# A projection that starts on the raw input: three half tiles summed from x before the norm is known, and scaled afterwards

## The reference, cut to what matters

```python
h = rmsnorm(x, norm_mix)                      # y = x * rsqrt(mean(x*x) + eps) * g
proj = h @ w_in + b_in                        # 5 * 1024 output channels
conv_val, conv_gate, pool_in, gate_a, gate_b = split(proj, 5)
ya = conformer_conv_branch(conv_val, conv_gate, ...)   # gate, 31-tap causal conv, layer norm, silu, matmul
yb = pool_branch(pool_in, ...)                         # trailing means over 2/4/8/16 tokens, group matmul
x = x + (sigmoid(gate_a) * ya + sigmoid(gate_b) * yb) @ mix_w_out
x = x + gdfn(rmsnorm(x, norm_ffn), ...)                # gated MLP, 2816 channels
return rmsnorm(x, norm_final)
```

## Time and profile before

| what | value |
|---|---|
| runs | 1361.4 us median of 3 (1361.03 to 1363.41) |
| the profiled execution | 1362.16 us, its span 1360.3 us |
| granted clock of TensorE, mean | 0.99 of full speed |
| busy: TensorE, VectorE, ScalarE, GpSimd | 98%, 60%, 29%, 54% of the span |

### The profile page before, as it was taken

The page is one execution under the profiler, slowest core; times in us unless marked ns, Lnnn a source line. Parts: engine busy times, 40 slices in busy tenths (PEclk is TensorE's granted clock), DMA queues, the critical chain, the costliest instruction groups (busy, mean ns, idle before and its releaser), DMA issues.

```text
span 1360.3 us, 16021 instructions
## 1 busy us (share of the span) xinstructions
PE 1336.2 (98%) x6092; PEld 1113.2 (82%) x6092; DVE 810.5 (60%) x971; ACT 399.5 (29%) x555; POOL 739.3 (54%) x502
## 2 busy tenths in 40 slices
PE   7999999999999999999999999999999999999997
PEld 6888888888888788878887888888888888888887
DVE  6799899999574545545696555454555453320225
ACT  4311221211112551111244444444444433322210
POOL 5656446554453353356947887777877714434101
PEclk8999999999999999999998999999999999999998
DMA  5111111110111112344302222222222238531003
GB/s 194 63 47 54 39 47 47 47 47 32 47 55 40 45 47 80 121 136 143 139 32 93 93 93 92 79 77 79 94 78 93 80 126 304 187 108 62 0 1 124
DMA packets 32931, 114.47 MB, mean 84 GB/s; under 512 B 3040, under 2 KB 9184, under 8 KB 28768
## 3 DMA queue, kind: packets, MB, share of 16 engines
q1 hardware_dynamic: 29328, 104.12, 22.2%
q10 hardware_dynamic: 3536, 9.44, 2.0%
HBM read 93.62 MB, written 19.92 MB: 83 GB/s over the span
## 4 chain that ended last, share of the span: by engine, by line
PE 86%; DVE 5%; DMA 2%; issue 1%; POOL 1%; ACT 1%; SPq 0%; POOLq 0%; DVEq 0%; ACTq 0%
PE ps L1366 28%; PE ps L1367 28%; PE ps L1368 28%; DMA tmp<-g_kept 2%; DVE ga_r L1216 1%; DVE tmp L1126 1%; DVE raw L1222 1%; POOL w_lo L565 0%; PE ps L1420 0%; PE ps L1430 0%; DVE ga_r L1241 0%; DVE res L1209 0%; DVE res L1207 0%; DVE res L1206 0%; DVE res L1343 0%
## 5 line engine op out<-in xcount | busy, mean ns | idle before, releaser
L1366 PE MATMUL ps<-h_lo,w_hi 128*128 128x512 f32 (+1 forms) x972 | 375.9, 387 | 8.1 <-DVE h_lo L971 6.6
L1367 PE MATMUL ps<-h_hi,w_lo 128*128 128x512 f32 (+1 forms) x972 | 373.1, 384 | 0.0
L1368 PE MATMUL ps<-h_hi,w_hi 128*128 128x512 f32 (+1 forms) x972 | 373.1, 384 | 0.0
L478 POOL TENSOR_SCALAR w_hi<-raw 128x1024 fp32r<-128x1024 f32 x66 | 72.1, 1093 | 297.9 <-issue 241.5
L1366 PEld LDWEIGHTS ps<-h_lo,w_hi 128*128 128x128 f32 x972 | 184.6, 190 | 45.7 <-DVE h_lo L971 7.4
L1367 PEld LDWEIGHTS ps<-h_hi,w_lo 128*128 128x128 f32 x972 | 184.6, 190 | 35.6 <-issue 0.5
L1368 PEld LDWEIGHTS ps<-h_hi,w_hi 128*128 128x128 f32 x972 | 184.5, 190 | 35.3
L1366 PE MATMUL ps<-ga_r,w_hi 128*128 128x512 f32 (+1 forms) x428 | 166.7, 389 | 4.0 <-POOL w_lo L565 3.0
L480 POOL TENSOR_TENSOR w_lo<-raw,w_hi 128x1024 fp32r<-128x1024 f32 x66 | 163.6, 2478 | 5.5
L1367 PE MATMUL ps<-cv_r,w_lo 128*128 128x512 f32 (+1 forms) x428 | 165.8, 387 | 0.0
L1368 PE MATMUL ps<-cv_r,w_hi 128*128 128x512 f32 (+1 forms) x428 | 165.8, 387 | 0.0
(11 more groups left out here) (193 smaller groups left out, 2011.7 us busy)
## 6 DMA issues: line engine op xcount, KB each, us to landing
raw<-in_wstream SPq DMA_DIRECT2D x68, 512.0 KB, 3.5
tmp<-in_wffn SPq DMA_DIRECT2D x16, 1024.0 KB, 4.8
tmp<-g_kept SPq DMA_DIRECT2D x22, 512.0 KB, 4.3
res<-in_wffn SPq DMA_DIRECT2D x10, 1024.0 KB, 4.7
g_kept<-res SPq DMA_DIRECT2D x14, 512.0 KB, 2.6
raw<-in_wffn SPq DMA_DIRECT2D x5, 1024.0 KB, 5.0
res<-in_xT ACTq DMA_DIRECT2D x4, 1024.0 KB, 4.9
x_kept<-res ACTq DMA_DIRECT2D x16, 256.0 KB, 2.3
```

The source lines that it names most:

```text
L478: pool.tensor_scalar(hi, r, 1.0, 0.0, ALU.mult, ALU.add).then_inc(w_hi_done, 1)
L1366: nc.tensor.matmul(out, a_hi, b_lo, start=start, stop=False, skip_group_check=onto)
L1367: nc.tensor.matmul(out, a_lo, b_hi, start=False, stop=False, skip_group_check=onto)
L1368: return nc.tensor.matmul(out, a_hi, b_hi, start=False, stop=stop, skip_group_check=onto)
```

## The change

What it does:

- **Raw first halves.** For tokens 0 to 511 (half 0, as quarters 0 and 1) ScalarE writes `h_hi` as x times gain (no factor), and VectorE `h_lo` as x times gain minus that, in one instruction with x and `h_hi` as inputs. TensorE makes the first halves of v0 and g0 (quarter by quarter) and of v1 from these. v1 goes to PSUM slot 2 (banks 4 and 5), so that three tiles stand open.
- **Scaling afterwards.** When the factor of half 0 is known, ScalarE copies it from PSUM to SBUF (`scales_kept`), and VectorE multiplies the three finished half tiles in PSUM by it.
- **The norm by halves.** Squares are taken by 1024 columns at a time and added in a tree of three (1024, 512 and 256 columns) for each quarter, all on VectorE, in the order of quarters 0, 2, 3, 1. Then half 1 is normed first, with 512 columns in an instruction, x in place in `res`; VectorE writes low halves of even k, GpSimd of odd k. Half 0 is normed later, when its raw halves have been used, for all tiles from g1 on. Its high halves of k = 4 to 7 stand behind the read-outs of g0 and v0 on ScalarE.
- **Weights.** GpSimd splits four chunks at the start, the third and fourth into `ga_r`. SyncE loads W0 before x, W2 and W3 once `raw` is free; the gain comes over ScalarE's DMA queue.
- **Order.** TensorE: v0, g0 on quarter 0; on quarter 1; v1 on half 0; v0 and g0 together on half 1; v1 on half 1; g1. The variances and broadcasts lie in between. The dummy matmuls are 16 instead of 24 and 6. The convolution waits for v1's read-out as well, since v1 lies in its banks. GpSimd's low halves of both norms come before glu0.

The diff, cut to its core:

```diff
+        n1_sq = [t[:, i * KT * PART:(i + 1) * KT * PART] for t in (tmp, cv) for i in range(2)]
+        n1_scale = [bank(6 + h) for h in range(2)]
+        scales_kept = cv[:, 5 * SEQ:5 * SEQ + HALF]
+        N_FIRST = 4
+        def first_w(n):
+            if n < 2:
+                return w_hi[:, n * CH:(n + 1) * CH], w_lo[:, n * CH:(n + 1) * CH]
+            a = (n - 2) * 2 * CH
+            return ga_r[:, a:a + CH], ga_r[:, a + CH:a + 2 * CH]
...
+            load_weights(0)
             load_x(0)
+            load_weights(1)
             load_x(1)
             load_x(2)
+            sp.wait_ge(w_split, 1)
+            load_weights(2)
             load_x(3)
             sp.dma_start(par[:, KT:], params[:, KT:]).then_inc(par_loaded, 16)
+            sp.wait_ge(w_split, 2)
+            load_weights(3)
...
-            for n in range(2):
-                split(n, n, 0)
+            for n in range(N_FIRST):
+                pool.wait_ge(raw_loaded[n % 2], 16 * (n // 2 + 1))
+                r, (hi, lo) = raw[:, n % 2 * CH:(n % 2 + 1) * CH], first_w(n)
+                pool.tensor_scalar(hi, r, 1.0, 0.0, ALU.mult, ALU.add).then_inc(w_hi_done, 1)
+                pool.wait_ge(w_hi_done, n + 1)
+                pool.tensor_tensor(lo, r, hi.bitcast(f32), ALU.subtract).then_inc(w_split, 1)
...
+            for h in (1, 0):
+                low_halves(n1[h], *span(h), None)
             for n in range(2, 2 * LOOSE):
-                split(n, n % 2, n // 2)
+                if n >= N_FIRST:
+                    split(n, n % 2, n // 2)
                 for x in BESIDE.get(n, ()):
                     beside(x[:-1], int(x[-1]))
...
+            def high_raw(p):
+                for k in range(KT):
+                    act.wait_ge(x_loaded[p][k * len(x_loaded[p]) // KT], 16)
+                    act.activation(tile(h_hi, k, *part(p)), tile(res, k, *part(p)), ACT.Copy,
+                                   scale=par1("norm_mix", k)).then_inc(raw_hi, 1)
...
+            high_raw(0)
+            squares(0)
+            high_raw(1)
+            for p in (2, 3, 1):
+                squares(p)
+            deviation(n1[1], 0, n1_scale[1])
             for k in range(KT):
+                high1(1, k)
+                if k == 4:
+                    deviation(n1[0], 8, n1_scale[0])
+            act.activation(small[:, 62:63], eps[:, :], ACT.Sigmoid).then_inc(gate_ready, 1)
+            act.wait_ge(bc_done, n1[0]["nth"])
+            act.activation(scales_kept, n1_scale[0], ACT.Copy).then_inc(scale_kept, 1)
+            act.wait_ge(raw_used, 1)
+            for k in range(KT // 2):
+                high1(0, k)
...
+            act.wait_ge(par_loaded, 16)
+            gate(0, TURN["g", 0], CHUNK["g", 0])
+            value(0, CHUNK["v", 0])
+            for k in range(KT // 2, KT):
+                high1(0, k)
+            act.wait_ge(n1[0]["lo_v"], KT // 2)
+            act.wait_ge(n1[0]["lo_p"], KT // 2)
+            act.dma_start(pw_raw, pool_w).then_inc(pw_loaded, 16)
+            for kind, i in START[2:]:
...
+            low_raw(0)
+            list(add_up(0, 0))
+            low_raw(1)
+            list(add_up(2, 1))
+            list(add_up(3, 2))
+            rest = add_up(1, 3)
+            next(rest)
+            invert(n1[1], 0, n1_diag[1])
+            list(rest)
+            normed(1, 4, lambda: invert(n1[0], 8, n1_diag[0]))
+            dve.wait_ge(scale_kept, 1)
+            dve.wait_ge(raw_used, 1)
+            for i in range(2):
+                scale(i)
             for c in range(2):
                 for odd in range(2):
                     a = c * GLW + odd * (PAD + HALF)
                     dve.memset(tmp[:, a:a + PAD], 0.0).then_inc(pads, 1)
+            normed(0)
+            scale(2)
+            for h in range(2):
+                settled(n1[h], True)
+            dve.wait_ge(par_loaded, 16)
             dve.memset(csum, 0.0).then_inc(pads, 1)
...
+                if isinstance(c, int) and c == 0:
+                    dve.wait_ge(val_out, 2)
                 dve.wait_ge(glu_done, 2 * c + 2)
...
+            keep_busy(16)
+            for p in range(2):
+                for n in range(2):
+                    pe.wait_ge(w_split, n + 1)
+                    for k in range(KT):
+                        pe.wait_ge(raw_lo, KT * p + k + 1)
+                        last = first(n, k, slot(n, *part(p)), *part(p))
+            last.then_inc(s1_half, 1)
+            pe.wait_ge(w_split, 3)
+            for k in range(KT):
+                if k == 3:
+                    variance1(1)
+                if k == 7:
+                    broadcast1(1)
+                last = first(2, k, slot(2, *span(0)), *span(0))
+            last.then_inc(raw_used, 1)
+            for k in range(KT):
+                if k == 2:
+                    variance1(0)
+                if k == 6:
+                    broadcast1(0)
+                low1(1, k)
+                for n in range(2):
+                    last = first(n, k, slot(n, *span(1)), *span(1))
+                    if k == KT - 1:
+                        last.then_inc(w_used, 1)
```

More of the change, by code:

```diff
@@ L333, in build @@
         n2_sq, n2_sum = sems("n2_sq", "n2_sum")
-        n2 = [norm(PARTS + 1 + h, ("val", "hi", "lo_v", "lo_p")) for h in range(2)]
+        n2 = [norm(3 + h, ("val", "hi", "lo_v", "lo_p")) for h in range(2)]
         x1_loaded = sem("x1_kept_most")
@@ L348, in build @@
         x2_mm, x2_done, last_gain, last_scale, last_out = sems("x2_mm", "x2_done", "last_gain", "last_scale", "last_out")
-        nf = [norm(PARTS + 3 + h, ("sq", "sum", "out")) for h in range(len(FINAL))]
+        nf = [norm(5 + h, ("sq", "sum", "out")) for h in range(len(FINAL))]
         x1_kept = nc.dram_tensor("x1_kept", (KT * P, SEQ), f32, kind="Internal").ap()
@@ L474, in split @@
                 pool.wait_ge(raw_loaded[s], 16 * (i + 1))
-                wait(pool, w_used, n - 1)
+                wait(pool, w_used, n - 3 if isinstance(n, int) and n < N_FIRST + 2 else n - 1)
                 pool.sem_inc(split_go, 1)
@@ new lines, in squares, with high1 @@
+            def squares(p):
+                act.wait_ge(x_loaded[p][-1], 16)
+                for q in range(2):
+                    x = res[:, 4 * q * SEQ:4 * (q + 1) * SEQ].rearrange("p (k n) -> p k n", k=4)
+                    a, b = part(p)
+                    act.activation(n1_sq[p][:, 4 * q * PART:4 * (q + 1) * PART].rearrange("p (k n) -> p k n", k=4),
+                                   x[:, :, a:b], ACT.Square).then_inc(squared, 1)
+            def high1(h, k):
+                act.wait_ge(n1[h]["val"], k + 1)
+                act.activation(tile(h_hi, k, *span(h)), tile(res, k, *span(h)), ACT.Copy).then_inc(n1[h]["hi"], 1)
@@ L626, in _ @@
+            act.dma_start(par[:, 0:KT], params[:, 0:KT]).then_inc(gain_loaded, 16)
             act.wait_ge(consts, 5)
             root_table()
[L628 to L643 removed]
+            act.wait_ge(gain_loaded, 16)
@@ L1439, in _, with variance1, broadcast1 @@
             pe.wait_ge(consts, 5)
-            def variance1(p):
-                squares = n1_sq[p % 2]
-                variance(bank(6 + p % 2), [((n1[p]["sum"], 5 if p == 0 else KT - 1), squares[0])], var_done, PART // P)
-            def broadcast1(p):
-                if p >= 2:
-                    pe.wait_ge(n1[p - 2]["val"], KT)
-                broadcast(n1[p], bank(4 + p % 2, 0, PART), n1_diag[p])
+            def variance1(h):
+                pe.wait_ge(tree, 12 - 3 * h)
+                for j in range(HALF // P):
+                    src = n1_sq[2 * h + j // 2][:, j % 2 * P:(j % 2 + 1) * P]
+                    last = nc.tensor.matmul(n1_scale[h][:, j:j + 1], src, mean_w[:, 0:1], start=True, stop=True)
+                last.then_inc(var_done, 1)
+            def broadcast1(h):
+                broadcast(n1[h], n1_scale[h], n1_diag[h])
             def keep_busy(n):
@@ new lines, in _ @@
+            for k in range(KT):
+                last = first(2, k, slot(2, *span(1)), *span(1))
+            last.then_inc(w_used, 1)
+            turn = TURN["g", 1]
+            pe.wait_ge(w_split, N_FIRST)
+            for h in range(2):
+                pe.wait_ge(s1_out, 2 * turn + h - 1)
+                for k in range(KT):
+                    if h == 0:
+                        low1(0, k)
+                    last = first(N_FIRST - 1, k, slot(1, *span(h)), *span(h))
+                last.then_inc(w_used if h else s1_half, 1)
```

149 lines of the change are left out of this document (45 added, 104 removed).

## The result

The changed kernel took 1366.81 us (median of 9 runs, 1364.37 to 1370.71), the kernel before, on the same chip, 1361.61 (9 runs, 1359.77 to 1364.54). The ratio is 1.0036, 95% interval 1.0023 to 1.0050: 3.1 to 6.8 us slower. The profiled execution has a span of 1366.5 us against 1360.3.

What follows compares the result with a forecast made beforehand. TensorE, busy 98%, bounds the kernel. The 3.4 us gained at p0 are lost in p2's wait, leaving p2 1.25 us later; 2.8 us of low clock make +4.1: from 1361.4 to 1365.5 us, range 1357 to 1369.

Steps and rivals of the forecast that it cites:

- Splits and held low halves: Front: GpSimd's weight splits hold Vector's raw low halves of quarter 1 until 25.2 us; alone they would end about 15.
- First broadcast: After v1's first half: done at 38.2 us with TensorE at 1.2 GHz for this piece, 34.9 at full clock.
- From there to the convolution: Second broadcast to first convolution: waits in a row on three in-order engines, 17.9 us; convolution at 68.3, 10 us later.
- p0: Start of tile p0: TensorE waits 2.5 us for GpSimd's split and starts at 71.9, 3.4 us earlier than before.
- p2: Start of tile p2: TensorE idles 4.7 us for g2's read-out, starting at 120.1, 1.25 us later than before.
- The clock behind p2: After the wait at p2: TensorE's clock falls to 0.50, costing 2.8 us.
- Nothing later: After p2: later places have room and waits from 420 us on move with TensorE, so no further cost.
- Rival 1: Front gain stays: late Vector chain hides in its room, p2 does not wait, 3.4 us kept; 1358.0; chance 0.10.
- Rival 2: GpSimd's hold of Vector is smaller: convolution at 61.8, p2 at 113.6; 1356.1, or 1358.9 with low clock; chance 0.13.
- Rival 3: Kinder clock: v1's first half at full clock, convolution at 65.0; 1359.3, or +0.7 us; chance 0.27 including its second form.
- its second form: Clock falls already at p0's 2.5 us wait, hidden by p2's wait: +1.25 us, 1362.7; chance included in Rival 3's.
- Rival 4: One more clock fall, under second halves of v0 and g0: convolution at 71.1, +6.9 us, 1368.3; chance 0.15.

Runs made afterwards that it cites:

- the first experiment: Changed kernel with ScalarE making the high halves of the pooled means behind g2's read-out, against the kernel before: 1361.73 us, ratio 0.9997.

## Why the prediction was right, and where its sizes were off

I forecast 1365.5, slower, with 0.50 for slower; it is 1366.8. Step by step:

- **Splits and held low halves.** Forecast ends of the splits: 8.0, 12.8, 20.1, 24.6; measured 8.2, 12.6, 19.8, 24.7. Last raw low half 25.4 (forecast 25.2), last sum 30.07 (30.3). The hold is as costed.
- **First broadcast.** Forecast end 38.2, of which 3.3 was a low clock under v1's first half; measured 37.07. The step failed in its place and size: the clock was down from 25.8 to 29.2, under g0's quarter 1, and at 1.00 while v1's first half ran (30.3 to 37.4). Among executions of this same front the broadcast's start ranges from 34.39 to 36.05 with the place of the low stretch, so such a fall costs up to 1.7 here. That the pauses lower the clock at all was right: with them filled it stayed up.
- **Second halves, second broadcast.** Idle 1.6 forecast, 1.53 measured; the broadcast ends at 49.84 (50.4). No clock fall came here.
- **From there to the convolution.** Forecast 17.9, measured 67.74 - 49.84 = 17.9.
- **p0.** Forecast 71.9 after a wait of 2.5; measured 71.11 after 1.92, 4.3 us earlier than the 75.42 of before (forecast 3.4, from 75.3).
- **p2.** Forecast a wait of 4.7 at 120.1 for g2's read-out; measured 4.37 at 119.32. From the convolution 51.58 (51.8), with the second mean held as foreseen. The term is 0.38 instead of 1.25: p2 came 0.8 earlier than forecast, most of it from the clock in the front, and the p2 of before is at 118.94, not at the 118.85 that the forecast worked out.
- **The clock behind p2.** 2.8 forecast; 3.06 - 0.38 = 2.7 measured, and by the dummies 2.6. The size is that of this execution: behind the same wait it was 1.4 in the run with `pads` at 4.
- **Nothing later.** This step failed in the profiled execution: I wrote that later places have room and that the last waits, from 420 us on, move with TensorE. The variance of the layer norm waits 0.67 where it waited 0.35, and a low clock of 6.8 us behind it cost 3.2. Of the nine profiles of the changed kernel and its variants with that wait of 0.67 us, three have a fall there (6.8, 3.4 and 3.4 us long); of the five with one of 0.35, the kernel before and its variants among them, two have one of 3.4. So it comes in some executions, whatever the kernel, and is no sure cost of the change. The sum without it, 0.4 + 2.7 + 0.3 = 3.4, lies at the lower end of the measured interval, 3.1 to 6.8.

  What fills the rest of the median's 5.2 stays open; that it is more such falls is argued, not shown. The same gap stands in other runs: the run with 20 dummies is 0.9 ahead of the kernel before at the wait for line 581 (728.03 against 728.89), and its median is 2.6 behind. One profile is one execution, and those of the variants lie from 3.9 below to 2.9 above their own medians, so rows of single profiles do not settle differences smaller than that. One more wait is new, 0.56 us for `res` at 756.94, and costs nothing that shows: between the wait for line 581 and the next one for it both kernels take 436.7 and 436.6 us.

The mechanism was right: the held low halves, the late convolution, ScalarE's order, the wait at p2 and the clock behind it all came as forecast, and the first experiment shows that the wait at p2 decides. That the time came out within 1.3 us of the forecast is in part luck. In the profiled execution p2 was 0.9 less late than forecast, and the later fall, put at nothing, more than made up for it.

Rival 1 failed as the forecast said, at ScalarE's order: the front gain was 4.3 at p0 and gone at p2. Rival 2, a smaller hold, was tried: without the hold the convolution starts at 64.09, not at 61.8, because the squares' sums take the low halves' place beside the splits. The rival had priced them as not held. Rival 3 came true in its place (v1's first half at 1.00) and not in its price, since the clock was down under g0 instead; its second form, the clock falling at p0, was seen in one variant's profile. Rival 4 did not come.

## What to carry to other kernels

A gain at the start passes every in-order queue before it counts: list the first waits that it runs into (here GpSimd's split at p0, ScalarE's read-out at p2) and take all of them away, since one removed alone may uncover the next (here another split, 1.6 us late). When one engine holds another, moving the holder can just move the hold to the next instructions, as it did here, where those had no time to spare. A loss of 0.36% and a gain of 0.3 to 0.4% lay three lines of order apart. And let medians decide before rows: the nine executions of the changed kernel lie 6.3 us apart, more than any single edit was worth.

## What the runs showed of the hardware

- A Vector instruction of 16 columns with two SBUF inputs lasted 2.33 us beside a GpSimd instruction of 2.42 us; 0.18 us with none beside it (at 110.18). It ended 0.03 us after the GpSimd instruction: the holder set the length of the hold, not the size of the held one. With the second input in PSUM eight low halves beside a split took 3.22 us, with both in SBUF 7.28. It goes both ways: beside Vector's sums GpSimd's two splits took 9.1 us instead of 7.0.
- Six profiles have the front of the changed kernel with its six pauses of up to 1.9 us. All six show the lower clock in it, but not at a fixed place: with the same instructions it was down from 25.8 to 29.2 in one execution, 13.7 to 17.1 in another, and in both places (12.6 to 16.0, 26.2 to 29.6) in a third. Its cost hangs on what TensorE does there: nothing where a wait for data behind it takes the lost time up, 1.7 us where TensorE is behind.
- Dummy matmuls in a wait (4.6 us of them in one of 4.4; 5.0 us spread over five waits; 17 us over the same five) had the clock at 1.00 in those waits and behind them, in each of the three kernels that had them. They must be sized by their own duration: a float32 matmul of 128 columns counted 0.24 us, and a list of them more than three times too long cost 6 us.
